# Down projection: twelve low parts built by ScalarE and an accumulating transfer instead of VectorE, and one more pair of weight tiles by seven products

## What is computed

```python
h = rmsnorm(x, g_ffn[l])
u = causal_dwconv(h @ w_up[l], ffn_conv_w[l]) + ffn_conv_b[l]
gate, val = jnp.split(u, 2, axis=-1)
x = x + (jax.nn.silu(gate) * val) @ w_down[l]     # (256 x 5632) @ (5632 x 2048)
return rmsnorm(x, g_final)
```

## Time and profile before

| | |
|---|---|
| median of 3 runs | 1912.88 us (1912.69 to 1913.09) |
| the profiled execution, its own time | 1912.82 us |
| its span in the profile | 1910.9 us |
| TensorE busy | 1901.6 us, 100% of the span |
| VectorE busy | 1420.2 us, 74% |
| ScalarE busy | 1069.9 us, 56% |
| GpSimd busy | 49.5 us, 3% |
| granted clock of TensorE, mean | 0.999 |

### The profile page before, as it was taken

The page is one execution under the profiler, slowest core; times in us unless marked ns, Lnnn a source line. Parts: engine busy times, 40 slices in busy tenths (PEclk is TensorE's granted clock), DMA queues, the critical chain, the costliest instruction groups (busy, mean ns, idle before and its releaser), DMA issues.

```text
span 1910.9 us, 26919 instructions
## 1 busy us (share of the span) xinstructions
PE 1901.6 (100%) x9951; PEld 1623.9 (85%) x9951; DVE 1420.2 (74%) x1956; ACT 1069.9 (56%) x1570; POOL 49.5 (3%) x72
## 2 busy tenths in 40 slices
PE   9999999999999999999999999999999999999998
PEld 7888898888888898888888888888888888888886
DVE  7777675656877675656768766888878878889898
ACT  6554676555555685654644444555555555555554
POOL 1000030000000030000100000000000000000000
PEclk9999999999999999999999999999999999999999
DMA  9864555566765455555666455656665666665664
GB/s 348 301 214 136 154 157 154 165 209 182 221 200 166 145 184 159 165 157 186 210 193 186 152 175 178 187 177 195 195 191 187 187 187 191 192 222 192 200 198 170
DMA packets 260362, 361.37 MB, mean 189 GB/s; under 512 B 15504, under 2 KB 159072, under 8 KB 259760
## 3 DMA queue, kind: packets, MB, share of 16 engines
q1 hardware_dynamic: 258400, 353.15, 58.7%
q0 software_dynamic: 1584, 6.67, 1.0%
q10 hardware_dynamic: 288, 0.33, 0.1%
HBM read 356.95 MB, written 3.16 MB: 188 GB/s over the span
## 4 chain that ended last, share of the span: by engine, by line
PE 99%; DMA 0%; ACT 0%; DVE 0%; SPq 0%; issue 0%; DVEq 0%; ACTq 0%
PE acc L478 22%; PE acc L471 12%; PE acc L455 10%; PE acc L456 10%; PE acc L457 10%; PE acc L1297 3%; PE acc L1571 3%; PE acc L1569 3%; PE acc L1570 3%; PE acc L1276 3%; PE acc L1277 3%; PE acc L1275 3%; PE acc L1300 2%; PE aux L548 1%; PE acc L498 1%; PE aux L1571 1%
## 5 line engine op out<-in xcount | busy, mean ns | idle before, releaser
L418 DVE TENSOR_TENSOR sb_w_lo<-sb_stage,sb_w_hi 128x1024 fp32r<-128x1024 f32 x476 | 582.3, 1227 | 286.2 <-ACT sb_w_hi L413 279.4
L413 ACT ACTIVATE sb_w_hi<-sb_stage 128x1024 fp32r<-128x1024 f32 x476 | 502.6, 1058 | 388.5 <-PE acc L457 123.9
L478 PE MATMUL acc<-sb_xT,sb_w_hi 128*128 128x512 f32 x1856 | 445.7, 391 | 0.0
L478 PEld LDWEIGHTS acc<-sb_xT,sb_w_hi 128*128 128x128 f32 x1856 | 340.8, 188 | 65.8
L471 PEld LDWEIGHTS acc<-sb_xT,sb_w_lo 128*128 128x128 f32 x1856 | 238.7, 191 | 9.3
L471 PE MATMUL acc<-sb_xT,sb_w_lo 128*128 128x256 f32 x1856 | 243.0, 283 | 0.0
L455 PE MATMUL acc<-sb_w_hi,sb_mT 128*128 128x512 f32 x480 | 190.4, 397 | 0.0
L456 PE MATMUL acc<-sb_w_lo,sb_mT 128*128 128x512 f32 x480 | 187.1, 390 | 0.0
L457 PE MATMUL acc<-sb_w_hi,sb_mT 128*128 128x512 f32 x480 | 187.0, 390 | 0.0
L455 PE MATMUL acc<-sb_w_hi,sb_xT 128*128 128x512 f32 x384 | 153.6, 400 | 0.0
L456 PE MATMUL acc<-sb_w_lo,sb_xT 128*128 128x512 f32 x384 | 149.7, 390 | 0.0
(11 more groups left out here) (488 smaller groups left out, 2999.0 us busy)
## 6 DMA issues: line engine op xcount, KB each, us to landing
sb_stage<-w_in SPq DMA_DIRECT2D x232, 512.0 KB, 4.3
sb_stage<-w_up SPq DMA_DIRECT2D x176, 512.0 KB, 3.6
sb_stage<-w_out SPq DMA_DIRECT2D x96, 512.0 KB, 4.0
sb_stage<-w_down SPq DMA_DIRECT2D x54, 512.0 KB, 6.6
sb_pair_stage<-w_down SPq DMA_DIRECT2D x34, 512.0 KB, 4.9
sb_kvb<-w_in SPq DMA_DIRECT2D x16, 512.0 KB, 6.4
sb_stage<-w_ukv SPq DMA_DIRECT2D x16, 512.0 KB, 4.3
sb_stage<-w_kv SPq DMA_DIRECT2D x15, 512.0 KB, 6.5
```

The source lines that it names most:

```text
L413: act.activation(w_hi[:, j % RING, 0:size], stage[:, j % RING, 0:size], ACT.Copy).then_inc(hi_ready, 1)
L418: dve.tensor_tensor(w_lo[:, j % RING, 0:size], stage[:, j % RING, 0:size], w_hi[:, j % RING, 0:size].bitcast(F32), ALU.subtract).then_inc( ...
L478: mm = pe.matmul(acc[:, 2 * pair + c, :], hi[:, k, c * P:(c + 1) * P], both, start=first and k == 0, stop=last and k == 3)
```

## The change

The list of the first half gets pair 8 as a ninth pair of seven (before, it was a plain pair at the end of the half). Twelve row units are "negated": the odd chunk of pairs 12 to 17 in each half. For them VectorE makes no low part. ScalarE, right after the high part, writes minus the high part into the low slot, and GpSimd issues a transfer that reads the unit's weights from HBM again and adds them to the slot (accumulating), which gives weight minus high part. TensorE waits for that transfer (`rest_moved`) instead of `lo_ready`; VectorE's next unit raises `lo_ready` by two. The first two of the four sums of a pair of seven become one instruction of 1024 columns, in the down projection and in the first block's input projection. The final gain goes to the other slot of `pair_stage`, as there are now 18 pairs of seven.

```diff
@@ -139,7 +139,7 @@
 OUT_PAIRS = [0, 1, 2, 6, 7, 3, 4, 5]
 
 SEVEN, LATE = 7, 2
-DOWN_PAIRS = [[[9, 10, 11], 0, [12], 1, [13], 2, [14], 3, [15], 4, [16], 5, [17], 6, [18], 7, [8, 19, 20, 21]],
+DOWN_PAIRS = [[[9, 10, 11], 0, [12], 1, [13], 2, [14], 3, [15], 4, [16], 5, [17], 6, [18], 7, 8, [19, 20, 21]],
               [[9, 10], 0, [11], 1, [12], 2, [13], 3, [14], 4, [15], 5, [16], 6, [17], 7, 8, [18, 19, 20, 21]]]
 
 
@@ -165,6 +165,8 @@
 DOWN_ROWS = [j for j, unit in enumerate(DOWN) if unit[0] == "rows"]
 SEVEN_FIRST = [j for j, unit in enumerate(DOWN) if unit[0] == "seven0"]
 DOWN_RING = 6
+NEGATED = [j for j, (kind, k, c) in enumerate(DOWN) if kind == "rows" and c % 2 == 1 and 12 <= k < 18]
+SECOND_FIRST = min(j for j in SEVEN_FIRST if DOWN[j][2] == 1)
 
 
 QKV_ITEMS = 2 * [[[2, 3, 4], 0, [5], 1, [6, 7]]]
@@ -365,6 +367,7 @@
         sum_ready, tap2_done = sem("sum_ready"), sem("tap2_done")
         gate_conv, gate_silu, act_ready = sem("gate_conv"), sem("gate_silu"), sem("act_ready")
         pair_staged = [sem("pair_staged0"), sem("pair_staged1")]
+        negated, rest_moved = sem("negated"), sem("rest_moved")
         sums_ready, first_copied, seven_free = sem("sums_ready"), sem("first_copied"), sem("seven_free")
         qkv_pair_staged = [sem("qkv_pair_staged0"), sem("qkv_pair_staged1")]
         qkv_sums_ready, mixed_ready = sem("qkv_sums_ready"), sem("mixed_ready")
@@ -715,7 +718,7 @@
         late.close()
         ffn_tmp = sb("ffn_tmp", [P, 4, 2, SEQ])
         half3, sum3, gate, value = (ffn_tmp[:, i, :, :] for i in range(4))
-        gfin = pair_stage[:, 1, :, :].rearrange("p a n -> p (a n)")
+        gfin = pair_stage[:, 0, :, :].rearrange("p a n -> p (a n)")
         rb3 = turn_f32[:, 1, 0:T * P].rearrange("p (t k) -> p t k", t=T)
         rbc3 = turn_f32[:, 1, T * P:T * P + SEQ]
         act_T = sb("act_T", [P, FT, 2, SEQ], F32R)
@@ -783,19 +786,27 @@
             act.wait_ge(unit_used, U4 + max(0, j - DOWN_RING + 1))
             src, hi, _ = down_parts(j)
             act.activation(hi, src, ACT.Copy).then_inc(hi_ready, 1)
+            if j in NEGATED:
+                act.activation(lo_of(j), src, ACT.Copy, scale=-1.0).then_inc(negated, 1)
+
+        def lo_of(j):
+
+            return down_parts(j)[2]
 
         def rest_down(step, dve, j):
 
 
+            if j in NEGATED:
+                return
             dve.wait_ge(hi_ready, U4 + (j + 1))
             src, hi, lo = down_parts(j)
-            dve.tensor_tensor(lo, src, hi.bitcast(F32), ALU.subtract).then_inc(lo_ready, 1)
+            dve.tensor_tensor(lo, src, hi.bitcast(F32), ALU.subtract).then_inc(lo_ready, 2 if j - 1 in NEGATED else 1)
             if DOWN[j][0] == "seven1":
                 pair = pair_stage[:, (sevens_until(j) - 1) % 2, :, :]
                 b11, b22, b12, b21 = pair[:, 0, 0:512], pair[:, 0, 512:UNIT], pair[:, 1, 0:512], pair[:, 1, 512:UNIT]
                 dve.wait_ge(lo_ready, U4 + (j + 1))
-                step(dve.tensor_tensor(b11, b11, b12, ALU.add))
-                dve.tensor_tensor(b12, b12, b22, ALU.add).then_inc(sums_ready, 1)
+                dve.tensor_tensor(pair[:, :, 0:512], pair[:, 0, :].rearrange("p (a n) -> p a n", a=2), again(b12, 2),
+                                  ALU.add).then_inc(sums_ready, 1)
                 dve.wait_ge(sums_ready, 2 * sevens_until(j) - 1)
                 step(dve.tensor_tensor(b22, b11, b22, ALU.add))
                 dve.tensor_tensor(b21, b22, b21, ALU.add).then_inc(sums_ready, 1)
@@ -863,8 +874,8 @@
                 pair = qkv_pair(n)
                 b11, b22, b12, b21 = pair[:, 0, 0:512], pair[:, 0, 512:UNIT], pair[:, 1, 0:512], pair[:, 1, 512:UNIT]
                 dve.wait_ge(lo_ready, base + (j + 1))
-                step(dve.tensor_tensor(b11, b11, b12, ALU.add))
-                dve.tensor_tensor(b12, b12, b22, ALU.add).then_inc(qkv_sums_ready, 1)
+                dve.tensor_tensor(pair[:, :, 0:512], pair[:, 0, :].rearrange("p (a n) -> p a n", a=2), again(b12, 2),
+                                  ALU.add).then_inc(qkv_sums_ready, 1)
                 dve.wait_ge(qkv_sums_ready, 2 * n + 1)
                 step(dve.tensor_tensor(b22, b11, b22, ALU.add))
                 dve.tensor_tensor(b21, b22, b21, ALU.add).then_inc(qkv_sums_ready, 1)
@@ -1081,6 +1092,13 @@
                 for i, (tile_, p0, n) in enumerate(sum(POOL_PIECES, [])):
                     pool.dma_start(pool_w[p0:p0 + n, i, :], w_rows[tile_ * P + p0:tile_ * P + p0 + n, :])\
                         .then_inc(mix_loaded, 16)
+
+                for n, j in enumerate(NEGATED):
+                    _, i, c = DOWN[j]
+                    pool.wait_ge(negated, n + 1)
+                    pool.dma_start(lo_of(j).rearrange("p (k n) -> p k n", n=512),
+                                   w_down2[:, 2 * i:2 * i + 2, c * 512:(c + 1) * 512], accum_op=ALU.add)\
+                        .then_inc(rest_moved, 16)
 
                 pool.wait_ge(lo_ready, U4 + (SEVEN_FIRST[-2] + 4))
                 pool.dma_start(gfin[:, :], dram["g_final_2"].partition_broadcast(P)).then_inc(gfin_loaded, 16)
@@ -1573,7 +1591,10 @@
                 def product_down(j, first, last):
 
                     _, i, c = DOWN[j]
-                    pe.wait_ge(lo_ready, U4 + (j + 1))
+                    if j in NEGATED:
+                        pe.wait_ge(rest_moved, 16 * (NEGATED.index(j) + 1))
+                    else:
+                        pe.wait_ge(lo_ready, U4 + (j + 1))
                     for k in range(2):
                         for t in range(T):
                             mm = passes(acc[:, 2 * (c % 2) + t, :], lambda h: act_T[:, 2 * i + k, h, t * P:(t + 1) * P], j, k,
@@ -1613,9 +1634,9 @@
                             banks_free(pe, PAIRS4, c)
                         product_down(j, first, j == DOWN_END[c])
                     if kind == "seven0":
-                        if j == SEVEN_FIRST[SEVEN + LATE - 1]:
+                        if j == SECOND_FIRST:
                             pe.wait_ge(seven_free, 1)
-                        product_seven(j, j in (SEVEN_FIRST[0], SEVEN_FIRST[SEVEN + LATE - 1]), j + 3 == SEVEN_END[c])
+                        product_seven(j, j in (SEVEN_FIRST[0], SECOND_FIRST), j + 3 == SEVEN_END[c])
                 for t in range(T):
                     o = acc[:, 2 + t, :]
                     for j in range(DOWN_TAIL, U_DOWN):
```

## The result

The changed kernel takes 1964.04 us (median of 5 runs, 1958.14 to 1965.81), the kernel before 1912.88 us: a ratio of 1.0262, 95% interval 1.0251 to 1.0273. The forecast was 1930 us with a range to 1962. The profiled execution took 1964.63 us, its span is 1961.7 us, 50.8 more than before.

The account below looks back on a forecast made before the run. TensorE's matmul count times their distance was taken as the bound. From 1912.82 us, - 0.7 (ninth pair) + 18.0 (twelve stalls) gave 1930 us; likeliest case 1920 to 1948, 8 in 10 from 1911.8 to 1962 us.

Parts of the forecast that it names:

- The bound and the matmuls: Down projection: TensorE never waits, so time is matmuls times distance; one matmul fewer gives 0.2267 us.
- VectorE's relief: Twelve subtractions (14.7 us) and about 5 us of sums leave VectorE; the path waits on none, worth 0.
- The ninth pair: First half of the down projection: 24 matmuls become 21, minus 0.7 us, with no other cost.
- that covers it: End of the first half: 6 row units (16.3 us) instead of 8 suffice for adding the sevens to x.
- The new wait: TensorE stalls for the accumulating transfer at each of twelve negated units: 1.5 us each, 18.0 us in all.
- its window: Time from the transfer's issue to TensorE wanting the unit, 4.8 us; every us beyond stalls TensorE.
- So 6.3 us: Accumulating transfer, issue to landing: 5.3 us from the nearest row plus 1.0 us, a 1.5 us stall per unit.
- 1.0 us for company: Added to the transfer's landing for sharing the DMA engines with SyncE's 2 MB burst.
- each stall lets the burst run out before the transfer: Reason for adding only 1.0 us, under half of the 2.3 us by which w_down's loads land later.
- The rival that it is dear: Transfers land in 8.3 to 10.6 us: 3.5 to 5.8 us a unit, 1954 to 1982 us; chance 0.22.
- Its sign, a landing over 8 us: What the transfers' own rows in the changed kernel's profile would show if accumulating is dear.
- the window case: Rival: transfers land in 4.4 to 4.8 us, TensorE never waits, 1912.1 us; chance 0.24 for fitting or nearly.

Follow-up runs that it names:

- the first kernel with the burst behind the transfer: The changed kernel with SyncE's 2 MB burst held until the accumulating transfer before it had landed, pairs loaded one row later: 1948.55 us (ratio 1.0192).
- the copy: The changed kernel with its twelve GpSimd transfers overwriting the low slot, without the add: 1951.59 us (ratio 1.0200).

## Why the prediction was wrong

- **The bound and the matmuls.** Right. TensorE's list is the time; VectorE's relief was worth nothing that the runs can tell: 1913.32 us with six early negated units, 1913.05 us with none.
- **The ninth pair.** Its sign was wrong by itself: "that covers it" failed at the change of halves, where six row units are too few for the adds in VectorE's list. That is 2.0 us of waits without negated units, 0.3 in the changed kernel. Why so little there is open: stalls that give VectorE time do not explain it, as the first kernel with the burst behind the transfer has one of 5.94 us just ahead and still waits 1.23 us for L542.
- **The new wait.** The mechanism was right: its place, its twelve times and, nearly, its window (4.6 us in the mean, 4.8 predicted). A transfer alone misses this window by 1.6 us, so about 12 x 1.6 = 19 of the 41.5 us would be there without any burst (an estimate).
- **The step that failed is the landing, "So 6.3 us"**: 5.3 us from the nearest row plus 1.0 us for company. TensorE's next weight load came 8.0 us after the issue in the mean, and the waits sum to 41.5 us instead of 18.0. Both terms were too small. The transfer alone took 6.2 us, not 5.3, which is about 11 of the missing 23.5 us; GpSimd's issue alone is 1.2 us, not the 0.5 of its plain ones. Company cost 1.8 us in the mean, not 1.0, about 10 us more; the shorter window gives the rest.
- **The reason given for the 1.0 us failed too**, that "each stall lets the burst run out before the transfer". It held after the waits of 6.9, 4.9, 6.6 and 3.5 us: the next transfer landed in 6.2 to 6.4 us. But the one behind that, issued some 4 us after the next burst, took 7.5 to 8.2 us in three of four cases (6.3 in the fourth), one behind that again 9.7 or 9.9 us; and the first of each half, with no stall ahead, had a burst before it and one behind, 11.5 and 10.4 us. Company costs up to 5.4 us (11.5 against 6.1).
- **A term was missing**: the clock that falls in or after the long waits, 9.7 us by the account above. Without it the range, to 1962 us, would have held the time.
- The rival that it is dear named 42 to 70 us and 1954 to 1982 us, and the time is in it. Its sign, a landing over 8 us, holds for five of the twelve. Of its two reasons the burst was the one that counted ("up to 10.6 in the burst"), not the many pieces of the add: the copy has the same 256 pieces, lands alone in 4.0 us and still costs 39 us.
- Two of its figures do not follow from its own sum, though the miss does not rest on them: 1 us a unit gives 1924 us, not 1920, and the window case is 1912.1, not 1911.8.
- The Trainium skill's rule of two source reads (Collectives: The Full Stack, The bandwidth ceiling) agrees with the transfers alone: 6.1 us with the add, 4.0 without, 3.5 for half the bytes. The Trainium skill's fit of 3.2 us (DMA: Bandwidth & Descriptors, Anatomy of one DMA) does not: no transfer of 512 KB by GpSimd landed in under 4.0 us.

## What to carry to other kernels

Before work is handed to a transfer, put its landing beside the time between the last use of its target and the next one, and the landing in company at that: here one that took 6 us alone took up to 11.5 us beside a queue that sends 2 MB at a go. If it does not fit, start it earlier into another buffer: here that turned 24 us for six transfers into less than one, while slowing the competing loads or shrinking the transfer left most of the loss. A relieved engine is worth only what the path waits for it, and saved matmuls can be eaten by the order of a list at the next change of stage.

## What the runs showed of the hardware

An accumulating transfer of 512 KB into SBUF by GpSimd took 1.2 us to issue and 6.1 us to land alone, a plain one 0.7 and 4.0 us. Beside a burst of 2 MB from SyncE's queue they took up to 11.5 and 10.6 us. TensorE's granted clock fell to 0.50 in a wait of 6.9 us and was still there for its next eleven matmuls, at a distance of 0.43 us. It fell to 0.50 after waits of 3.0 and 3.5 us as well, with TensorE already busy again; after waits of 1.5 to 1.9 us, and one of 2.9 us, the windows show no fall.
